# Experts of a three-block model: hidden rows turned in 32x32 blocks on VectorE, down weights loaded by quadrants, beginning and S5 loads reordered

## The reference

```python
D_FF_EXPERT = 1408                       # N_EXPERTS = 8, TOP_K = 2
def swiglu(x, w1, w3, w2):
    return (jax.nn.silu(x @ w1) * (x @ w3)) @ w2

def moe_swiglu(x, w_router, b_router, w1, w3, w2):
    logits = (xt @ w_router) + b_router
    top_v, top_i = lax.top_k(logits, TOP_K)
    gates = jax.nn.softmax(top_v, axis=-1)
    dense_gate = jnp.sum(jax.nn.one_hot(top_i, N_EXPERTS) * gates[..., None], axis=1)
    for e in range(N_EXPERTS):
        y = y + dense_gate[:, e:e + 1] * swiglu(xt, w1[e], w3[e], w2[e])
```

## Time and profile before

| | |
|---|---|
| median of 3 runs | 1446.78 us (1445.71 to 1449.45) |
| the profiled execution | 1451.63 us, span 1449.8 us |
| PE busy | 1347.9 us, 93% of the span |
| DVE, ACT, POOL busy | 366.1, 243.6, 181.9 us |
| moved by DMA | 292.65 MB, mean 202 GB/s |
| longest waits of PE | 22.4 us for a norm after the experts, 17.6 us (13 times) for `moe_w` in L2030 |

### The profile page before, as it was taken

The page is one execution under the profiler, slowest core; times in us unless marked ns, Lnnn a source line. Parts: engine busy times, 40 slices in busy tenths (PEclk is TensorE's granted clock), DMA queues, the critical chain, the costliest instruction groups (busy, mean ns, idle before and its releaser), DMA issues.

```text
span 1449.8 us, 23908 instructions
## 1 busy us (share of the span) xinstructions
PE 1347.9 (93%) x10525; PEld 895.2 (62%) x10525; DVE 366.1 (25%) x796; ACT 243.6 (17%) x548; POOL 181.9 (13%) x137
## 2 busy tenths in 40 slices
PE   6998999999999979997999999888848989999997
PEld 5887996877777747445544554344326646776673
DVE  0635644251253064224000000000022152000001
ACT  2342232121010102411110111011011021000000
POOL 1020000407567000000200000000334000000000
PEclk9999999999999989997999999999978989999999
DMA  9424010796433762837999999999989240433520
GB/s 319 151 82 145 2 59 0 211 373 227 154 111 120 94 175 41 329 133 268 388 326 339 395 345 325 370 360 328 356 254 329 75 163 1 156 134 116 199 91 29
DMA packets 111116, 292.65 MB, mean 202 GB/s; under 512 B 6412, under 2 KB 41328, under 8 KB 111056
## 3 DMA queue, kind: packets, MB, share of 16 engines
q1 hardware_dynamic: 98128, 259.93, 53.4%
q0 software_dynamic: 4944, 15.19, 3.6%
q10 hardware_dynamic: 7984, 16.65, 3.5%
HBM read 274.58 MB, written 17.17 MB: 201 GB/s over the span
## 4 chain that ended last, share of the span: by engine, by line
PE 75%; SPq 11%; DMA 6%; DVE 4%; ACT 2%; issue 2%; POOL 0%; ACTq 0%; DVEq 0%; POOLq 0%
PE bank L1551 23%; PE bank L2030 8%; PE bank L2173 8%; PE bank L1564 6%; PE bank L2056 5%; PE bank L1850 4%; PE bank L1978 4%; DMA arena<-moe_w 3%; PE bank L1528 3%; SPq L537 3%; PE bank L1557 2%; SPq L528 2%; PE bank L1904 2%; SPq L534 2%; SPq L529 2%
## 5 line engine op out<-in xcount | busy, mean ns | idle before, releaser
L1551 PE MATMUL bank<-xT,arena 128*128 128x256 f32 x1696 | 378.5, 383 | 5.1 <-DMA arena<-gdn_w_in 2.3
L1551 PEld LDWEIGHTS bank<-xT,arena 128*128 128x128 f32 x1696 | 323.1, 192 | 56.8 <-issue 8.1
L2030 PE MATMUL bank<-arena 128*32 128x352 f32 x3072 | 233.6, 462 | 18.6 <-DMA arena<-moe_w 17.6
L2030 PEld LDWEIGHTS bank<-arena 128*32 128x32 f32 x3072 | 101.5, 110 | 148.4 <-issue 113.4
L2056 PE MATMUL bank<-arena 128*32 128x256 f32 x2112 | 116.4, 380 | 3.0 <-DMA arena<-moe_w 3.0
L2173 PE MATMUL bank<-arena 128*128 128x512 f32 x256 | 111.0, 592 | 0.0
L2056 PEld LDWEIGHTS bank<-arena 128*32 128x32 f32 x2112 | 67.4, 110 | 49.5 <-DMA arena<-moe_w 4.9
L2173 PEld LDWEIGHTS bank<-arena 128*128 128x128 f32 x256 | 48.6, 190 | 58.2 <-issue 57.9
L1528 PE MATMUL bank<-const,arena 128*128 128x128 f32 (+1 forms) x432 | 57.3, 276 | 29.2 <-DVE arena L1154 22.4
L1138 DVE TENSOR_TENSOR arena<-arena,bank 128x352 f32<-128x352 f32 x24 | 12.5, 522 | 241.8 <-PE bank L2030 241.8
L1528 PEld LDWEIGHTS bank<-const,arena 128*128 128x128 f32 (+1 forms) x432 | 47.7, 143 | 40.1 <-DVE arena L1154 22.8
(11 more groups left out here) (345 smaller groups left out, 1272.5 us busy)
## 6 DMA issues: line engine op xcount, KB each, us to landing
arena<-moe_w SPq DMA_DIRECT2D x64, 1408.0 KB, 24.3
arena<-ffn_w SPq DMA_DIRECT2D x33, 1024.0 KB, 10.2
arena<-moe_w SPq DMA_DIRECT2D x32, 1024.0 KB, 20.3
arena<-gdn_w_in SPq DMA_DIRECT2D x8, 2048.0 KB, 9.9
arena<-w_up SPq DMA_DIRECT2D x8, 2048.0 KB, 8.3
arena<-w_down SPq DMA_DIRECT2D x8, 2048.0 KB, 7.7
slot_rows<-arena ACTq DMA_DIRECT2D x1, 9600.0 KB
arena<-moe_w SPq DMA_DIRECT2D x24, 384.0 KB, 20.9
```

The lines of the kernel that those rows point to most:

```text
L1551: last = mm(bank[:, at:at + SEQ], w[:, k, P * m:P * m + P], x[:, k, :], start=(k == 0), stop=(k == KT - 1))
L2030: last = mm(banks[i][32 * q:32 * q + 32, 0:EW1], xg[:, EK * s + kk, 32 * t:32 * t + 32], w[:, kk, EW1 * q:EW1 * q + EW1], start=(s == 0 an ...
```

## The change

1. Experts. `mh` is 352 wide; DVE transposes it in 32 x 32 blocks (`V_.transpose`) right behind each product. PE's three transposes per group and ACT's five copies are gone, and with them the semaphore between the two. In `mhT`, partition 32 q + r and column 32 x + i now hold token i and inner row 352 q + 32 x + r, so the down weights for block x must lie with row 352 q + 32 x + r in partition 32 q + r. They are loaded in 11 transfers per expert, each 4 quadrants x 32 rows of 4 KB into 128 partitions. The source is written with the quadrant as its outermost dimension (4), then the 32 rows.
2. Beginning. SP loads the identity alone, x, the first slab of `gdn_w_in`, the rest of the constants, the other slabs, without waiting for POOL. POOL's gate columns wait for x; its norm weights wait for `in_tile` 8. PE's gate product moves behind `in_product(3)`, ACT's gate functions behind the first four tiles.
3. S5. The two halves of `s5_w_in` are issued before the table loads, as soon as the last SwiGLU up product is done. The tables of pieces 0 to 2 are waited for together.
4. Small ones. The memset of `mh` is gone; ACT, not POOL, waits for the last stored rows before the last fetch, and POOL's dummy instruction there is gone.

```diff
@@ block.sync
-            sp.dma_start(const[:], A["shape_const"].rearrange("p (a b) -> p a b", b=P)).then_inc(const_loaded, 16)
+            ident_in = A["shape_const"].rearrange("p (a b) -> p a b", b=P)
+            sp.dma_start(const[:, 0:1], ident_in[:, 0:1]).then_inc(x_loaded, 16)
             sp.dma_start(xres[:], A["x"][0].rearrange("(n p) d -> p n d", p=P)).then_inc(x_loaded, 16)
...
-            sp.wait_ge(vecs_loaded, 48)
-            sp.wait_ge(ba_w_loaded, 16)
             for b in range(8):
...
                 load(sp, ("gdn_in", b), b % 4, region(4096 * (b % 4), KT, 512), w_in[:, :, 512 * b:512 * b + 512])
+                if b == 0:
+                    sp.dma_start(const[:, 1:N_CONST], ident_in[:, 1:N_CONST]).then_inc(const_loaded, 16)
...
+            sp.wait_ge(up_done, 2 * FC * FF_CHUNKS)
+            for c in range(2):
+                load(sp, ("s5_in", c), 7 + c, s5_in_w[c], rows(A["s5_w_in"][0], 4 * c, 4))
             sp.wait_ge(kz_stored, 64)
             sp.wait_ge(xrow_loaded, 16)
-            sp.wait_ge(up_done, 2 * FC * (FF_CHUNKS - 2))
             sp.wait_ge(down_done, FF_CHUNKS - 2)
             for j in range(NPIECE - 1):
                 table_loads(j)
-            sp.wait_ge(up_done, 2 * FC * FF_CHUNKS)
-            for c in range(2):
-                load(sp, ("s5_in", c), 7 + c, s5_in_w[c], rows(A["s5_w_in"][0], 4 * c, 4))
+            sp.wait_ge(t_loaded, 32 * SUB * (NPIECE - 1))
             sp.wait_ge(u_done, 4)
             table_loads(NPIECE - 1)
...
-                    w2q = w2e[:, EW1 * q:EW1 * q + EW1].rearrange("e f d -> (e f) d")
-                    sp.dma_start(m2[q][:, 0:2], w2q[0:2 * P].rearrange("(b p) d -> p b d", p=P)).then_inc(m_loaded[EC + q], 16)
-                    if q < EC - 1:
-                        f0 = EW1 * EC - ER + 32 * q
-                        sp.dma_start(m2[q][0:ER, 2], w2q[2 * P:EW1]).then_inc(m_loaded[EC + q], 16)
-                        sp.dma_start(m2[q][ER:P, 2], w2e[:, f0:f0 + 32].rearrange("e f d -> (e f) d")).then_inc(m_loaded[EC + q], 16)
+                    for b in range(3 if q < EC - 1 else 2):
+                        f0 = 32 * (3 * q + b)
+                        sp.dma_start(m2[q][:, b], w2e.rearrange("e (s f) d -> s (e f) d", s=EC)[:, f0:f0 + 32]).then_inc(m_loaded[EC + q], 16)
@@ block.gpsimd
+            pool.wait_ge(x_loaded, 32)
             pool.dma_start(region(38984, KT, 16), A["gdn_w_in"][0].rearrange("(k p) f -> p k f", p=P)[:, :, 4096:4112]).then_inc(ba_w_loaded, 16)
...
-            pool.wait_ge(m_y, n_pass * (EXPERTS * (EC + 2)))
-            pool.wait_ge(y_stored, n_pass * (64 * EXPERTS) + 64)
-            link(nc.gpsimd.tensor_tensor(pool_pad, zero_c, zero_c, ALU.add))
+            pool.wait_ge(routed, 4)
@@ block.vector
-            link(V_.memset(mh, 0.0))
...
-                    V_.tensor_tensor(mh[:, t, 0:EW1], msil[:, t], banks[2 * t + 1][:, 0:EW1], ALU.mult).then_inc(m_h, 1)
+                    V_.tensor_tensor(mh[:, t], msil[:, t], banks[2 * t + 1][:, 0:EW1], ALU.mult).then_inc(m_h, 1)
+                    dve.wait_ge(m_h, k * ST + t + 1)
+                    V_.transpose(mhT[:, t], mh[:, t]).then_inc(m_hT, 1)
@@ block.tensor
-                pe.wait_ge(m_h, k * ST + 2)
-                hidden(0)
-                hidden(1)
+                pe.wait_ge(m_hT, k * ST + 1)
                 pe.wait_ge(xrow_loaded, k * 16 + 32)
...
-                pe.wait_ge(m_h, k * ST + 3)
-                hidden(2)
...
-                        for b, m in ((0, c), (1, EC + c), (2, 2 * EC + c)):
-                            if m == FE_T:
-                                continue
+                        for x in range(3 * c, min(3 * c + 3, FE_T)):
                             for q in range(EC):
-                                last = mm(y_bank[t][32 * q:32 * q + 32, 0:EW2], mhT[:, m, t], m2[c][:, b, EW2 * q:EW2 * q + EW2],
-                                          start=(m == 0), stop=(c == EC - 1 and b == 1))
+                                last = mm(y_bank[t][32 * q:32 * q + 32, 0:EW2], mhT[:, t, 32 * x:32 * x + 32], m2[c][:, x % 3, EW2 * q:EW2 * q + EW2],
+                                          start=(x == 0), stop=(x == FE_T - 1))
```

More of the change, by code:

```diff
@@ L594, in norm_load @@
                 pool.dma_start(norm_w[:, slot, :], every(A[name], DM, off)).then_inc(normw_loaded, 16)
+            nc.gpsimd.memset(pre[:, :, 0:CONV - 1], 0.0).then_inc(pad_ready, 1)
+            pool.wait_ge(in_tile, 8)
             norm_load(0, "ln_g", 0)
             norm_load(1, "ln_b", 0)
-            nc.gpsimd.memset(pre[:, :, 0:CONV - 1], 0.0).then_inc(pad_ready, 1)
+            pool.wait_ge(const_loaded, 16)
             for j in range(4):
@@ L1260, in _, with gates @@
             take_x(1)
-            act.wait_ge(ba_v, 1)
-            link(A_(tmp_b, tmp_a, ACT.Abs, bias=zero_c))
-            link(A_(tmp_b, tmp_b, ACT.Exp, bias=zero_c, scale=-1.0))
-            A_(a_log, a_log, ACT.Exp, bias=zero_c).then_inc(ba_a, 1)
-            A_(tmp_b, tmp_b, ACT.Ln, bias=one_c).then_inc(ba_a, 1)
-            link(A_(beta, ba[:, :, 0:8], ACT.Sigmoid, bias=zero_c))
+            def gates():
+                act.wait_ge(ba_v, 1)
+                link(A_(tmp_b, tmp_a, ACT.Abs, bias=zero_c))
+                link(A_(tmp_b, tmp_b, ACT.Exp, bias=zero_c, scale=-1.0))
+                A_(a_log, a_log, ACT.Exp, bias=zero_c).then_inc(ba_a, 1)
+                A_(tmp_b, tmp_b, ACT.Ln, bias=one_c).then_inc(ba_a, 1)
+                link(A_(beta, ba[:, :, 0:8], ACT.Sigmoid, bias=zero_c))
             def decays():
@@ L1304, in _ @@
                         A_(root, banks[5][:, 0:256].rearrange("p (n a b) -> p n a b", n=NT, b=8)[:, :, :, 0], ACT.Sqrt, bias=eps_rms).then_inc(root_ready, 1)
-                if b:
+                if b == 0:
+                    gates()
+                else:
                     take_silu(b - 1)
@@ L1459, in _ @@
                 act.dma_start(xrow, slots[bass.ds(k + 1, 1)].rearrange("a s d -> (a s) d")).then_inc(xrow_loaded, 16)
-                def take_hT(t):
-                    act.wait_ge(m_tr, k * ST + t + 1)
-                    nc.scalar.copy(mhT[:, 0:2 * EC, t], banks[2 + t][:, 0:2 * P].rearrange("p (m i) -> p m i", i=32))
-                    nc.scalar.copy(mhT[0:ER, 2 * EC:FE_T, t], banks[2 + t][0:ER, 2 * P:3 * P - 32].rearrange("p (m i) -> p m i", i=32))
-                    for j in range(3):
-                        last = nc.scalar.copy(mhT[ER:P, 2 * EC + j, t], banks[2 + t][32 * j:32 * j + 32, 3 * P - 32:3 * P])
-                    last.then_inc(m_hT, 1)
                 for t in range(ST):
@@ L1471, in _ @@
                     A_(msil[:, t], banks[2 * t][:, 0:EW1], ACT.Silu, bias=zero_c).then_inc(m_sil, 1)
-                for t in range(ST):
-                    take_hT(t)
                 act.wait_ge(y_stored, k * 64 + 64)
@@ L1482, in _ @@
                                   ysb[32 * q:32 * q + 32]).then_inc(y_stored, 16)
+            act.wait_ge(y_stored, n_pass * (64 * EXPERTS) + 64)
+            act.sem_inc(routed, 1)
             def mean_square(n):
@@ L1574, in _, with gate_product @@
             need_x()
-            w_ba = region(38984, KT, 16)
-            pe.wait_ge(ba_w_loaded, 16)
-            for n in range(NT):
-                last = token_major(banks[6 + n][:, 0:16], xT, w_ba, n)
-            last.then_inc(ba_done, 1)
+            def gate_product():
+                w_ba = region(38984, KT, 16)
+                pe.wait_ge(ba_w_loaded, 16)
+                for n in range(NT):
+                    last = token_major(banks[6 + n][:, 0:16], xT, w_ba, n)
+                last.then_inc(ba_done, 1)
             def cumulated_g():
@@ L1642, in _ @@
             for m in range(24):
+                if m == 4:
+                    pe.wait_ge(const_loaded, 16)
+                    gate_product()
                 if m == 8:
@@ L2013, in _ @@
             with pe.Fori(0, n_pass * EXPERTS) as k:
-                def hidden(t):
-                    for b in range(3):
-                        last = transpose(four(banks[2 + t])[:, b], mh[:, t, P * b:P * b + P])
-                    last.then_inc(m_tr, 1)
                 pe.wait_ge(xg_ready, k * 2 + 2)
```

13 lines of the change are left out of this document (6 added, 7 removed).

## The result

The changed kernel takes 1770.75 us (median of 4 runs, 1763.07 to 1776.21); the kernel before, run beside it, took 1448.12 us (1445.71 to 1460.44). The ratio is 1.2203, 95% interval 1.2118 to 1.2288: **slower by 22%**. Some runs of a kernel here lie over 1.5% above its fastest; the ratios leave these out, the medians and ranges do not.

A forecast was written before the change was run, and what follows sets the result against it. PE was taken to bound the first half of the experts, the weight stream the second and the end. Down weights +399, beginning -2.3, S5 -7.7, small ones -0.3 sum to +389 on 1446.8: 1836 us, own range 1703 to 1969, whole range 1395 to 2030.

The forecast's parts named there:

- Four engines: Experts' down weights: the source's outer count of 4 leaves only four of 16 engines, 26.0 GB/s each; chance 0.78.
- The price, 72.1 us per expert: Experts' down weights: middle between 55.5 and 88.7 us per expert, against 22.2 before; +399 us in all.
- the low end: Experts' down weights: four engines at 26.0 GB/s each take 55.5 us per expert instead of 22.2; +266 us.
- Transposes, block transposes, ACT's copies: Experts: PE saves 0.95 us each where it is the bound, DVE's block transposes hidden, ACT's copies idle-time; worth 0.
- Beginning: Kernel start: PE's first tile begins earlier, at 13.7 instead of 20.04, and the gate product's 4.0 us return; -2.3 us.
- S5: S5 product: PE's two waits for `s5_w_in`, 3.53 and 4.14 us, go as its loads precede the tables; -7.7 us.
- Small ones: Memset's removal worth 0; dropping POOL's dummy instruction before the last fetch, with the signal over ACT, worth -0.3 us.
- Full rate: Experts' down weights on all 16 engines at 416 GB/s, 13.9 us per expert, PE the bound; 1403 us, chance 0.14.
- from 10 engines on it is faster, with 8 or fewer slower: Experts' weight stream with n engines changes by 8 x (222 / n - 22.2) us; edits before the experts bring 10.3.
- 16 engines, but uneven: Experts' down weights keep 22.2 us each on all 16 engines, only edits before the experts count; 1436 us, chance 0.06.

The follow-up runs named there:

- the run of the early edits: The kernel before with everything of the change but the experts (beginning, S5's order, POOL's and ACT's small edits): 1425.26 us, ratio 0.9876.

## Why the prediction was right, and what it mis-sized

**Four engines: right, with the row it named.** Share 0.25, 104 GB/s, and the run with contiguous rows shows that nothing else in the change costs time. The runs with 8 and 16 pieces and with hand-cut transfers leave the outer count as the cause. 5.77 MB at 4 x 26 GB/s gives 55.5 us; the second c alone confirms the rate (15.0 us for 1.57 MB).

**The price, 72.1 us per expert: too high.** The step was "I expect losses of this kind. I take the middle". The losses exist, but only for a part of the time, and I had charged half of the full loss over all of it. Four engines alone write at their full 26 GB/s; the loss comes only while the other twelve work at the next up slabs. Per expert each of the four carries 1.44 MB of down weights and 0.72 MB of up slabs, 83.2 us at 26 GB/s. In some 22 us of them (about 983 to 1005 above) it runs at 252 / 16 = 15.8 and loses 22 x (1 - 15.8 / 26) = 8.6. Together 91.8, measured 92.9. In the terms of the sum: eight times 55.5 - 22.2 is +266, and seven mixed stretches add 60. Behind the last expert's down weights no up slabs follow, but the third block's first loads do (L347, from 1355.41): 242 GB/s with a share of 1.03 from 1362 to 1365, and the last c comes 14.4 us behind the third instead of 10, 4 more. So some 330 of the measured +334.9 are explained; the rest was not traced further. The term was +399, too large by 64 us. That is most of the 77 us between the predicted +389 and the +311.4 of the two spans; the other 13 are the early edits and what lies behind the experts, below. (Between the medians the distance is 65, since the profiled execution after lies 7.7 us under its median and the one before 4.9 over the median that the forecast started from.) The measured +334.9 lies halfway: 69 above the low end, +266, which goes by the engines' own rate, and 64 below the middle. That the middle of a range from no loss to loss all the time came this close is in part luck, since the prediction had no row for how long the two kinds overlap. SP's issue does not run ahead of the data, which limits the overlap, and this could have been asked of SP's timeline before.

**Transposes, block transposes, ACT's copies: right.** 0.99 us per expert where PE is the bound (said 0.95), nothing under the forecast; the block transposes are hidden in both kinds of run.

**Beginning: right in kind, -5.3 instead of -2.3.** PE's timeline after:

```profile
13.00 14.05 PE L1548 MATMUL bank<-xT,arena 128*128 128x256 f32 x64 [0.92 <-DMA arena<-gdn_w_in]
26.88 3.64 PE L1561 MATMUL bank<-arena,xT 128*128 128x16 f32 x32
30.37 14.06 PE L1548 MATMUL bank<-xT,arena 128*128 128x256 f32 x64
44.27 0.29 PE L1584 MATMUL bank<-small,const 128*128 128x16 f32 x2
```

The tiles start at 13.00 instead of 20.04, 0.7 earlier than said, and 3.5 come back for the gate product. The other 1.8 are the clock: the eight tiles took 29.6 us before (20.04 to 49.61), with a granted clock of 0.52 from 20 to 24, behind PE's wait for the slab, and 1.00 from there, and 27.8 now, at 1.00 throughout. In the run of the early edits the clock was at 0.68 from 28 to 32 and at its lower level, 0.50, from 32 to 36, with PE shown busy throughout, and the second four tiles took 16.63 us instead of 14.06. So these 2 us vary between executions and are no sure gain.

**S5: right in kind, -10.4 instead of -7.7.** The two waits shrank by 6.9 us. The rest is again the clock. Windows of the kernel before:

```profile
520.00:525.00 5.00, 1.47 (x15) 0.86 (x19) 2.64 (x7) 0.54 (x1) 1.06 (x2) 0.71 1.03 409
525.00:530.00 5.00, 2.77 (x28) 1.08 (x20) 0.00 (x0) 0.00 (x0) 0.00 (x0) 0.50 1.01 398
530.00:535.00 5.00, 3.09 (x32) 1.47 (x36) 3.00 (x12) 0.00 (x0) 0.00 (x0) 0.50 0.02 8
```

The clock fell to the lower of its two levels (granted 0.50, 1.2 GHz) in the first wait (3.53 us, up to 524.12), and stayed there through the second one to 535, so the first 32 matmuls and some of the 480 behind them ran at half clock: 3.65 + 28.01 = 31.66 us for 512 matmuls. Now they take 28.17 without a break. I had priced the waits, not what they do to the clock behind them.

**Between S5 and the experts** lie the other 2.2 of the 17.95 us. Nothing was forecast for them: 1.2 are in one product (43.05 us at L1979, 44.27 before at L1978) that the change doesn't touch, the rest was not traced.

**Small ones: -0.3, measured -1.7** between the last down product and the next turn (20.64 us, before 22.36). But these edits are not shown to be the cause: the run of the early edits has them and 21.88, and the kernel before with even transfers hasn't and shows 18.88. The other 3.9 us behind it lie mostly in one product's clock (24.30 us now, 27.03 before).

**The rivals.** Full rate (1403) is what the contiguous rows give: 1398. The rule "from 10 engines on it is faster, with 8 or fewer slower" holds at 8 (1574), but its formula was too kind to eight engines: 8 x (222 / 8 - 22.2) = +44 us, 1480 with the early edits, a period of 55.7 us. Measured were 67.0 (831.73 to 898.74 in PE's timeline). Of the 11 us that are missing, 20 x (1 - 14.8 / 26) = 8.6 are again the mixed stretch, at 236 / 16 = 14.8 GB/s per engine; the rest stays open. The formula knew only the engines' number, not that they meet. "16 engines, but uneven" (1436) is nearly what 16 pieces of 8 rows do: 1451.

## What to carry to other kernels

Before a transfer's source is rearranged so that its partitions come in a few groups, look at the outermost dimension on both sides: here an outer count of 4 instead of 128 left 4 of 16 engines at work, with the same bytes and as few transfers. If the layout allows it, choose which rows go where so that each transfer is 128 consecutive rows, and let the matmul pick its columns; that cost PE nothing here and gave 27 us, 1.9%. Where the few engines can't be avoided, look at what runs beside them: a wait that kept the two kinds of load apart was worth 35 us. Two waits of PE at the start of a long product cost more than their length, 10.4 us and not 7.7, since the clock was still at its lower level behind them.

## What the runs showed of the hardware that I had not expected

- A transfer's rate depends on more than its number of engines. With all 16 busy, 128 outer rows run at 416 GB/s, 16 x 8 rows at 273, four times 32 partitions at 271. Four engines alone (105) or eight alone (210) lose nothing, and four of them beside twelve with even transfers bring all 16 down to 252. A possible reading is that adjacent partitions on one engine collide with the other engines' writes; that was only argued, since no view shows which partitions an engine writes, and no run separates the writing side from the reading one. The Trainium skill's page "SBUF — State Buffer", section "Door 1: The DMA port swizzle", says that a transfer to 32 partitions reaches 8 of 16 ports; an estimate from that is half of 416, 208 GB/s. Measured were 271, with several such transfers in flight, so the ports of a single transfer don't give the rate here.
- Uneven transfers weigh more than their bytes: with about a quarter of the down weights' bytes uneven, the kernel before had stretches of 20 us at 265 GB/s, and mending that quarter alone is worth 1.9%.
- The issue of eleven transfers of 512 KB took SP 59.98 us with four engines, as long as their data, 36.45 with eight, 25.37 with sixteen pieces, and 11.41 with contiguous rows. What stands behind such loads in SP's program is late by that much.
